# Joining the two split pairs of weight slabs in a feed-forward block, and splitting the next block's first slab earlier

## The reference, cut to what matters

```python
def swiglu(x, w_gate, w_up, w_down):
    return (jax.nn.silu(x @ w_gate) * (x @ w_up)) @ w_down      # 1024 -> 2752 -> 1024, float32

for l in range(DEPTH):                                          # DEPTH = 2
    x = x + hybrid_mixer(x, ...)
    h = rms_norm(x, norm_ffn[l])
    x = x + (swiglu(h, dense weights) if l == 0 else
             moe_ffn(h, ...))         # for each of 8 experts: swiglu of the tokens routed to it, times the router's weight
```

## Time and profile before

| | us |
|---|---|
| median of 3 runs | 1364.25 |
| the 3 runs | 1364.01, 1364.25, 1367.51 |
| the profiled execution's own time | 1366.55 |
| its span in the profile | 1364.7 |

### The profile page before, as it was taken

The page is one execution under the profiler, slowest core; times in us unless marked ns, Lnnn a source line. Parts: engine busy times, 40 slices in busy tenths (PEclk is TensorE's granted clock), DMA queues, the critical chain, the costliest instruction groups (busy, mean ns, idle before and its releaser), DMA issues.

```text
span 1364.7 us, 17430 instructions
## 1 busy us (share of the span) xinstructions
PE 1312.7 (96%) x6156; PEld 985.1 (72%) x6156; DVE 1142.6 (84%) x1233; ACT 878.4 (64%) x965; POOL 79.9 (6%) x61
## 2 busy tenths in 40 slices
PE   6999999999999999999999998999999999999998
PEld 5787778888887887788666776666766667666675
DVE  6988987654448889885998988999889998899998
ACT  4445556444435445645777778987789877798775
POOL 0020001000000110100060000000000000000400
PEclk9999999999999999998999999999999999999999
DMA  9353343965493435152999999999999999999996
GB/s 343 134 184 128 120 170 131 397 238 184 155 361 124 152 126 185 62 201 76 376 379 384 412 339 384 414 403 422 383 362 409 403 421 391 349 397 398 420 392 256
DMA packets 63316, 394.75 MB, mean 289 GB/s; under 512 B 6641, under 2 KB 7233, under 8 KB 23570
## 3 DMA queue, kind: packets, MB, share of 16 engines
q1 hardware_dynamic: 58610, 375.41, 70.9%
q10 hardware_dynamic: 2848, 11.53, 2.1%
q0 software_dynamic: 1792, 6.95, 1.5%
HBM read 376.44 MB, written 17.43 MB: 289 GB/s over the span
## 4 chain that ended last, share of the span: by engine, by line
PE 63%; DVE 20%; issue 5%; ACT 4%; DVEq 0%; POOL 0%; ACTq 0%
DVE w_lo L1193 14%; PE bank L1775 13%; PE bank L2077 13%; PE bank L1776 13%; PE bank L2054 9%; PE bank L1825 4%; ACT w_hi L793 3%; DVE ys L1182 1%; PE bank L1920 1%; PE bank L1788 1%; PE bank L2064 1%; PE bank L1820 1%; PE bank L2171 1%; DVE act L1587 1%; DVE tmp L1182 1%
## 5 line engine op out<-in xcount | busy, mean ns | idle before, releaser
L1193 DVE TENSOR_TENSOR w_lo<-raw,w_hi 128x2048 fp32r<-128x2048 f32 (+2 forms) x383 | 794.4, 2088 | 93.9 <-ACT w_hi L793 92.4
L793 ACT ACTIVATE w_hi<-raw 128x2048 fp32r<-128x2048 f32 (+2 forms) x383 | 669.8, 1755 | 128.8 <-PE bank L2077 58.0
L1775 PE MATMUL bank<-w_hi,hT_hi 128*128 128x512 f32 (+3 forms) x968 | 383.0, 396 | 2.7 <-DVE hT_lo L1182 1.6
L1776 PE MATMUL bank<-w_hi,hT_lo 128*128 128x512 f32 (+3 forms) x968 | 375.2, 388 | 0.0
L1775 PEld LDWEIGHTS bank<-w_hi,hT_hi 128*128 128x128 f32 (+1 forms) x968 | 170.2, 176 | 52.2 <-issue 5.2
L1776 PEld LDWEIGHTS bank<-w_hi,hT_lo 128*128 128x128 f32 (+1 forms) x968 | 170.3, 176 | 44.7 <-issue 1.0
L2054 PE MATMUL bank<-w_lo,hT_hi 128*96 128x512 f32 (+3 forms) x616 | 162.3, 388 | 0.8 <-DVE w_lo L1193 0.8
L2054 PEld LDWEIGHTS bank<-w_lo,hT_hi 128*96 128x96 f32 (+1 forms) x616 | 103.1, 169 | 37.4 <-DVE w_lo L1193 4.3
L1825 PE MATMUL bank<-w_lo,hT_hi 128*128 128x512 f32 x352 | 87.9, 392 | 0.4 <-DVE w_lo L1193 0.3
L2139 PE MATMUL bank<-w_lo,hT_hi 128*128 128x512 f32 (+1 forms) x264 | 78.0, 413 | 9.4 <-DVE w_lo L1193 9.4
L1006 ACT ACTIVATE act_hi<-bank 128x192 fp32r<-128x192 f32 (+1 forms) x66 | 24.8, 376 | 94.3 <-PE bank L2064 94.2
(11 more groups left out here) (281 smaller groups left out, 1350.1 us busy)
## 6 DMA issues: line engine op xcount, KB each, us to landing
raw<-in_moe SPq DMA_DIRECT2D x240, 1024.0 KB, 7.8
raw<-in_mix SPq DMA_DIRECT2D x56, 1024.0 KB, 4.8
raw<-in_dense SPq DMA_DIRECT2D x30, 1024.0 KB, 4.9
raw<-in_moe SPq DMA_DIRECT2D x16, 768.0 KB, 8.2
raw<-in_moe SPq DMA_DIRECT2D x12, 512.0 KB, 7.6
slot_h<-x_squared ACTq DMA_DIRECT2D x1, 5632.0 KB, 41.5
slot_y<-x_squared ACTq DMA_DIRECT2D x1, 5632.0 KB, 24.2
raw<-in_moe SPq DMA_DIRECT2D x8, 256.0 KB, 4.0
```

Of the source, the lines that this page charges most:

```text
L793: nc.scalar.activation(HI[:, split_slot, 0:width], RAW[:, raw_slot, half:half + width], ACT.Copy)\
L1193: vec.tensor_tensor(LO[:, split_slot, 0:width], RAW[:, raw_slot, half:half + width], HI[:, split_slot, 0:width].bitcast(F32), ALU.subtract ...
L1775: mm(out_, left[0], right[0], start=start, stop=False)
L1776: mm(out_, left[1], right[1], start=False, stop=False)
```

## The change

A block has 33 slabs, numbered 2 to 34. The four halves at its start become two whole slabs of 2048 columns (2 and 3), and the 1024 and 512 columns at its end become one slab of 1536 (34). So four `w_hi` and `w_lo` instructions of 1024 columns become two of 2048, and the 1024 and the 512 become one 1536, on ACT and on DVE, in each of the nine feed-forward blocks. The loads of the start were whole before; at the end one load of 768 KB replaces one of 512 and one of 256 KB. Every matmul of before is still there, the same number with the same shapes.

In PE's order all eight `w_hi` matmuls of a joined first slab now precede its four `w_lo` matmuls, where each half had its own four and two, and `add_y_lo` stands behind the first whole slab. At the end (`down_end`) all `act_hi` products of `w_hi` come first, then all `act_lo` products, then `w_lo`.

In wide blocks of layer 1 ACT splits the next block's first slab between the last silu and `turned_hi`, and DVE between the last `mult` and `turned_lo`. In narrow blocks it stays behind the turned tokens. In block 0 `take_y_light` stands behind slab 4's split, and waits one slab further; elsewhere its place, between the block's second and third slab of before, is kept.

In block 7 the ring skips three places (`LATE_SKIP`) and not two: the loads of slabs 19 to 21 wait for the `w_lo` of the slab three back (four before), those of 22, 23 and 24 for the slab nine back, and these three come in two pieces each.

```diff
-FFN_SLABS = 36
+FFN_SLABS = 33
+FFN_FIRST = 2
+FFN_END = FFN_FIRST + FFN_SLABS
-LATE_SLAB = 19
-REJOINED = (LATE_SLAB - 2 + RAW_SLOTS, LATE_SLAB - 1 + RAW_SLOTS)
+LATE_SLAB, LATE_SKIP = 19, 3
+REJOINED = range(LATE_SLAB + LATE_SKIP, LATE_SLAB + 2 * LATE_SKIP)
-FFN_WIDTHS = [4 * CHUNK] * 4 + [SLAB] * 27 + [8 * TAIL] * 2 + [SLAB, D, D // 2]
+FFN_WIDTHS = [SLAB] * 29 + [8 * TAIL] * 2 + [SLAB, D + D // 2]
 def back(p, late=False):          # the load of slab p waits for the w_lo of slab p - back
-    place = ffn_place(p, late)
-    if place < RAW_SLOTS:
-        return p + RAW_SLOTS - place
-    place -= 2 * RAW_SLOTS if late and p in REJOINED else RAW_SLOTS
-    return p - (2 * place + 1 if place < 2 else place if late and place >= LATE_SLAB else place + 2)
+    if late and p in REJOINED:
+        return RAW_SLOTS + LATE_SKIP
+    return RAW_SLOTS - LATE_SKIP if late and p < LATE_SLAB + LATE_SKIP else RAW_SLOTS
...
         # ACT, ffn_block (wide); DVE has the same with mult and turned_lo
                 turned_hi(qb + NCH - 1, 1)
-                ffn_split(34, at, n0, r0, D)
+                ffn_split(34, at, n0, r0, D + D // 2)
                 silu(qb + NCH, n0 + 32, 0, TAIL)
-                ffn_split(35, at, n0, r0, D // 2)
+                if is_moe:
+                    ffn_split(FFN_END, at, n0, r0)
                 turned_hi(qb + NCH, 0)
                 if is_moe:
-                    ffn_split(FFN_SLABS, at, n0, r0, 4 * CHUNK)
                     turned_tokens_hi(b + 1, CAP if spread or y_added is None else LCAP)
...
-                    ffn_split(FFN_SLABS + 1, at, n0, r0, 4 * CHUNK)
-                    ffn_split(FFN_SLABS + 2, at, n0, r0, 4 * CHUNK)
+                    ffn_split(FFN_END + 1, at, n0, r0)
         # PE, ffn_block
-                for part in range(4):
+                for part in range(2):
...
-                    if part == 1 and y_ready is not None:
+                    if part == 0 and y_ready is not None:
                         add_y_lo(y_ready)
         # PE, down_end: first term (tb: 128-row halves of the tokens; tbs = 1 in layer 1)
+                    for tb in range(tbs):
+                        tok = slice(tb * rows, (tb + 1) * rows)
+                        for half in range(2):
+                            mm(PS[4 + 2 * tb + half][0:rows, :], left[:, 0, tok], right[:, s, half * 512:half * 512 + 512],
+                               start=False, stop=False)
```

More of the change, by code:

```diff
@@ L83, in raw_place @@
-def raw_place(stage, p):
-    return PLACE[stage] + (p if stage[0] == "mix" else ffn_place(p))
-def raw_slot(stage, p):
-    return raw_place(stage, p) % RAW_SLOTS
-def raw_half(stage, p):
-    return p % 2 * 4 * CHUNK if stage[0] == "ffn" and p < 4 else 0
-def width_of(stage, p):
-    return FFN_WIDTHS[p % FFN_SLABS] if stage[0] == "ffn" else SLAB
-FFN_WIDTHS = [4 * CHUNK] * 4 + [SLAB] * 27 + [8 * TAIL] * 2 + [SLAB, D, D // 2]
-SLAB_AT = [P * sum(FFN_WIDTHS[:p]) for p in range(FFN_SLABS)] + [3 * FF * D]
@@ L106, in raw_value, with raw_place, raw_slot, width_of @@
-def raw_value(stage, p):
-    return 16 * (raw_place(stage, p) // RAW_SLOTS + 1)
+    return p - FFN_FIRST + (LATE_SKIP if late else 0)
+PLACE = FIRST
+def raw_place(stage, i):
+    return PLACE[stage] + i
+def raw_slot(stage, i):
+    return raw_place(stage, i) % RAW_SLOTS
+def width_of(stage, i):
+    return FFN_WIDTHS[i] if stage[0] == "ffn" else SLAB
+FFN_WIDTHS = [SLAB] * 29 + [8 * TAIL] * 2 + [SLAB, D + D // 2]
+SLAB_AT = [P * sum(FFN_WIDTHS[:i]) for i in range(FFN_SLABS + 1)]
+def raw_value(stage, i):
+    return 16 * (raw_place(stage, i) // RAW_SLOTS + 1)
@@ L966, in _ @@
                     split_to(first + 1, stage)
-                elif layer == 0:
-                    split_to(first + 2, stage)
             turned_h(2)
@@ L2383, in rows @@
         return down[c * CHUNK:(c + 1) * CHUNK].reshape(2, P, D).transpose(1, 0, 2).ravel()
-    found = [gate_up(2 * part, 2, slice(0, CHUNK)) for part in range(4)]
+    found = [gate_up(4 * part, 4, slice(0, CHUNK)) for part in range(2)]
     for c in range(1, NCH + 1):
```

192 lines of the change are left out of this document (90 added, 102 removed).

## The result

The changed kernel is slower. Its median is 1374.29 us of 5 runs (1371.72 to 1377.68) against 1366.97 for the kernel before in the same comparison (5 runs, 1364.01 to 1367.51): ratio 1.0063, 95% interval 1.0046 to 1.0080. I had forecast 1367.8, no change that can be measured, and a range from 1361.0 to 1371.5. Of the 6.5 us between forecast and measurement 2.7 are the starting point: the forecast added 3.55 to 1364.25, a median of 3 runs, and with two more runs the median of the kernel before is 1366.97. The other 3.8 are the forecast difference, 3.55 where the medians differ by 7.3. The profiled execution of the changed kernel took 1374.32, its span is 1372.5, 7.8 us longer than that of the profile of before.

A forecast was written before the change was run, and what follows sets the result against it. PE was taken to bound wide blocks, DVE and the weight stream narrow ones. Terms -0.8 + 0.3 + 0 + 2.25 + 1.0 + 0.8 = +3.55 us on the median of 1364.25 gave 1367.8, range 1361.0 to 1371.5.

The forecast's parts named there:

- Joining saves 157 and 151 ns of DVE work, worth nothing on the path: All expert blocks: joins save 0.465 us of DVE work each, 3.7 over eight, valued at 0 on the path.
- Start of block 0, -0.8: Block 0's start: DVE runs 1.1 us earlier with whole slabs, a gain of 0.8 (bounds 0.4 and 1.2).
- the seam behind it, +0.3: Seam from block 0 to 1: PE waits for a later act_lo, partly made up, +0.3 us (0 to 0.5).
- Seams from wide to narrow, 0: Three seams into narrow blocks, taken as bound by DVE and DMA: 0 us (bounds -0.3 and +0.8 each).
- Seams from narrow to wide, 3 x 0.75: Three seams into wide blocks: the first whole slab's w_lo comes late, +2.25 us (bounds 0.2 and 1.3 each).
- The ring, +1.0: Block 7: loads of slabs 19 to 21 are issued one w_lo later, PE waits, +1.0 us (bounds 0 and 3.4).
- The end of block 7, +0.8: End of block 7: act_lo comes 1.12 us later behind a longer w_lo, +0.8 us (bounds 0.4 and 1.2).
- C: Rival: joined seams from narrow to wide cost 1.6 us each, 2.5 more in all, 1370.3; chance 0.22.
- D: Rival: block 7's loads take 7.8 us, not 4.8, PE waits up to 3.4, +2.4, 1370.2; chance 0.14.
- B: Rival, faster: the joins' 3.7 us and block 0's 0.8 come back, late act_lo and seams hidden, 1359.8; chance 0.14.
- E: Rival: earlier preparation puts each of three narrow blocks 1.2 us ahead, -3.6 cancels the sum, 1364.3; chance 0.13.

The follow-up runs named there:

- e3_clock: The changed kernel with 8 + 8 matmuls of 256 columns added in each narrow block's opening to keep PE busy: 1368.98 us, ratio to before 1.0035.
- e5_before_clock: The kernel before with 8 + 8 matmuls of 256 columns added in each narrow block's opening: 1363.36 us, ratio to before 0.9992.
- e6_tail_busy: The kernel before with only the end joined (1536 columns, ring skipping three places) and busy matmuls in the narrow openings: 1371.50 us, ratio 1.0050.
- e4_heads_busy: The kernel before with only the first two pairs of halves joined, split unmoved, and busy matmuls in the narrow openings: 1374.93 us, ratio 1.0074.
- e2_ends: The changed kernel with the next block's first slab split behind turned_hi and turned_lo again in wide blocks: 1376.76 us, ratio to before 1.0086.
- e11_order: The changed kernel with the last slab's products reordered, all 128-row ones before all 64-row ones, no busy matmuls: 1371.54 us, ratio to before 1.0045.
- e12_tail_order_busy: e6_tail_busy with the last slab's 128-row products all ahead of its 64-row ones: 1365.82 us, ratio to before 1.0000.
- e9_order_busy: e3_clock with the last slab's 128-row products all ahead of its 64-row ones: 1367.88 us, ratio to before 1.0018.

## Why the prediction was wrong, step by step

**Joining saves 157 and 151 ns of DVE work, worth nothing on the path.** Right on the path: no block became shorter by it. The work that went is 2.6 us and not 3.7, since halves in a row overlapped (two in 2.36).

**Start of block 0, -0.8, and the seam behind it, +0.3.** The gain was half of mine, the loss more than twice mine. The -0.13 on the ruler is near the -0.5 by luck, as shown in the section on the result. In e3_clock, without a fall of the clock near, block 0's lead grew by 0.4 against e5_before_clock by its sixth chunk, my lower bound, and 0.7 was lost at the seam, above my upper bound of 0.5: +0.3 in sum where I had -0.5.

**Seams from wide to narrow, 0.** This is one step that failed, though 0.39 a seam lies within the bounds of -0.3 to +0.8. I wrote that "the block that follows is bound by DVE and DMA, which have the same work in another order". The measured term is 3 x 0.39 = 1.2. The share of DVE is a mean over the block; its opening is a chain through ACT, PE and DVE in which PE is late at once. The runs give the parts: what the end of a wide block loses by the alternation passes into it whole (0.65 to 0.67 a seam in e6_tail_busy), joined first slabs alone cost 1.23 (e4_heads_busy), and the moved split gives 0.83 back (e2_ends).

**Seams from narrow to wide, 3 x 0.75.** The size was right, 0.84, 0.84 and 0.87, and the chain that I forecast is one of two. The lines that answer to the earlier trace rows, in the changed kernel:

```profile
911.30 1.92 ACT L782 ACTIVATE w_hi<-raw 128x2048 fp32r<-128x2048 f32 x1
...
911.44 0.70 PE L2160 MATMUL bank<-w_hi,act_hi 128*128 128x512 f32 x2 [0.60 <-issue]
912.07 0.50 PE L2164 MATMUL bank<-w_hi,act_hi 64*128 64x512 f32 x2
...
913.25 2.29 DVE L1174 TENSOR_TENSOR w_lo<-raw,w_hi 128x2048 fp32r<-128x2048 f32 x1 [0.98 <-ACT w_hi L782]
...
913.59 0.48 PE L1749 MATMUL bank<-w_hi,hT_hi 128*96 128x512 f32 x1
...
915.59 1.18 PE L2030 MATMUL bank<-w_lo,hT_hi 128*96 128x512 f32 x4
...
916.61 0.62 PE L2220 MATMUL bank<-y_lo,swap 128*128 128x512 f32 x2
```

`w_hi` is there at 913.22 and the whole slab's `w_lo` at 915.54, the shift of 1.70 aside within 0.1 of the forecast. But PE starts only at 913.59, behind the last products of block 2. These begin 0.4 late, because the `w_lo` of 1536 columns now stands ahead of the low part of the narrow `act_hi` on DVE, and alternate between the kinds, which takes 2.15 us where it was 1.76. So PE reaches the `w_lo` products at 915.59, just when they are ready. Both chains end together: without the joined end the seam still costs 0.94 to 0.98 (e4_heads_busy), without the joined first slabs 0.64 to 0.68 (e6_tail_busy).

**The ring, +1.0.** The place and the late loads were right, the size in this trace 1.5. I counted one late load's way to `act_lo`; five are late. In the other kernels with this ring it is 0.5 to 2.2, so my 1.0 is inside what it can be.

**The end of block 7, +0.8.** Measured 0.9, but not as worked out. I priced "eight more matmuls of 0.23". The lines that answer to the earlier trace rows:

```profile
1360.95 0.71 PE L2072 MATMUL bank<-w_hi,act_hi 128*96 128x512 f32 x2
1361.59 0.47 PE L2078 MATMUL bank<-w_hi,act_hi 64*96 64x512 f32 x2
1362.21 0.69 PE L2072 MATMUL bank<-w_hi,act_lo 128*96 128x512 f32 x2
1362.83 0.47 PE L2078 MATMUL bank<-w_hi,act_lo 64*96 64x512 f32 x2
1363.23 0.71 PE L2072 MATMUL bank<-w_lo,act_hi 128*96 128x512 f32 x2
1363.87 0.48 PE L2078 MATMUL bank<-w_lo,act_hi 64*96 64x512 f32 x2
```

Two 64-row products together take 0.23 and not 0.46 (see the last section), and every change of kind costs 0.165. The two errors nearly cancel: from 1362.21 the eight take 2.1 to the end, where I had 1.84 and the latency. The wait for `act_lo`, priced at 0.38, is about 0.2: it is there at 1362.15, 1.1 later behind the transposes than before as forecast, and PE, slowed by the change of kind, is hardly ahead of it. Without the moved split 0.66 of the 0.9 stays (e2_ends), without the alternation 0.76 (e11_order). And e4_heads_busy, which has neither, ends 0.6 late too: DVE does the whole first slab that stands behind the block (1363.42 to 1365.71) ahead of its last copy.

**The clock: no term at all.** This is the other step that failed. In the profiles the fall in block 2 and the longer one in block 6 are 2.25 of the 4.2 us by which the sum of 3.55 fell short of 7.8, and with PE kept busy they are gone (e3_clock). I treated PE's idle time in the narrow opening as free. The earlier trace rows has the clock at 1.00 in both blocks, and nothing in them says how near the edge it is; the same profile has a fall in block 6, which I did not look for. What the clock is worth in the medians is less sure: 7.3 us with it, 5.6 in the pair e3_clock and e5_before_clock without it, and so 1.7, with intervals of about 2 us on each. Nor is the clock of the two profiles lower on one side only, since that of before fell ahead of block 0. What is missing without the clock, 4.9 in the profiles of that pair against my 3.55, is mainly the seams to narrow blocks at 0.3 each and block 0 with its seam at +0.3.

**The rivals.** C (seams to a wide block at 1.6) and D (loads at 7.8 us) did not come about; B and E neither. The outcome lay outside all of them, because I let no two small losses, and no loss of clock, add up.

## What to carry to other kernels

Where PE already waits in short pieces, price a later seam twice: once for the time, and once for what the wait may do to PE's clock; look for windows of a lower clock in the profile of before first. An instruction's place in an order written by hand costs also through the buffer that it needs: before moving a step forward, count how many steps back its slot was last used. Products of different heights are to be kept in groups; that pays where nothing else holds PE there (5.7 us in e12_tail_order_busy), and little where another wait ends at the same time (1.1 in e9_order_busy).
